# Letting an accumulating transfer make the low half of some weight pieces

## The chip, the cores and the metric

The kernel runs on one core of a Trainium2 chip. The metric is the device time of one execution in microseconds (us); three runs of the kernel as it stood took 2312.73, 2313.27 and 2313.78 us, so the time before is their median, 2313.27 us. The profile is a trace of one execution on that core.

## The reference

The program is a decoder trunk of two layers on 512 tokens of width 1024, all in float32. Each layer runs a half-step SwiGLU feed-forward, a token mixer (gated linear recurrence and differential attention in one layer, forgetting attention and a convolution in the other), cross-attention into 256 memory tokens, and a second feed-forward. Every sub-layer is normalised ahead and behind and added to the residual stream `h`. What matters here is the feed-forward:

```
def swiglu(x, w_gate, w_up, w_down):
    return (jax.nn.silu(x @ w_gate) * (x @ w_up)) @ w_down

def half_ffn(h, l, j):
    y = swiglu(rms_norm(h, ffn_norm_pre[l, j]), ffn_w_gate[l, j], ffn_w_up[l, j], ffn_w_down[l, j])
    return h + 0.5 * rms_norm(y, ffn_norm_post[l, j])
```

`w_down` is 2816 x 1024. There are four feed-forwards (two layers, two each).

## The kernel before

**Split products.** Every float32 matrix product is made of three products of rounded halves. A tensor X becomes a high part (X rounded to the `fp32r` format) and a low part (X minus the high part), and the result is high x low + low x high + high x high. So each weight piece goes through a small assembly line before TensorE (PE in the profile) can use it:

1. SyncE (the queue SPq) loads the raw piece, 128 partitions x 1024 floats (512 KB in two transfers of 256 KB), into one of 4 slots of `raw` (L541). It waits for the slot through the semaphore `lo_made`.
2. ScalarE (ACT) writes the rounded copy into one of 4 slots of `whi` (L791 for the pieces of this document), once the raw data is there and the piece that used the slot four pieces ago has been used by PE (`pieces_used`). It counts `hi_made`.
3. VectorE (DVE) writes raw minus high into `wlo` (L1319) and counts `lo_made`.
4. PE waits for `lo_made` (`weights`) and uses both; then it counts `pieces_used`.

ACT and DVE split three pieces ahead of the piece that PE is on (`LOOKAHEAD`). Each engine runs its own written-out order of work; the splits stand in it as calls of `split_next`.

**The plain down stage.** The feed-forward's down product is made in three stages; two use a fast block scheme, and the third, called `down` in the list of stages, is a plain product over the last 1280 rows of `w_down`. It has two groups (column halves of 512), each of 5 pieces. The document numbers its ten pieces 0 to 9: pieces 0 to 4 are the first group, 5 to 9 the second. A piece holds 2 x 128 rows; over the four token tiles it is 24 matmuls.

In the first group PE takes a piece for all four token tiles, then the next piece. In the second group (`last_group`) it takes piece 5 for all tiles, then pieces 6, 7, 8 and 9 for tile 0, then the same four for tile 1, then the rest. So pieces 6 to 9 are all wanted within one tile's time.

At the change of groups DVE runs `close_sublayer` in this order, one after the other: it waits until the first group is done, adds its four tiles to `y_rows` (L1460), splits piece 8, multiplies the four tiles by the gain (`gained`, L1471), splits piece 9, and then handles the second group's tiles as PE ends them. ACT splits piece 8, squares the four tiles (L841), and splits piece 9 once piece 5 is used. GpSimd (POOL) computes only reciprocal square roots in these stages (L692), each behind a wait.

Of the kernel before, what the change touches and what calls it, by code (L numbers as in the profile page):

```python
# [41 lines left out]
P = 128  # L42
# [7 lines left out]
RAW_SLOTS = 4  # L50
SPLIT_SLOTS = 4
# [39 lines left out]
def stages():  # L91

    out = []

    def ffn(l, j):
        for n, (_, ng) in enumerate(FF_GROUPS):
            out.append(("gate_up", l, (j, n), ng, KT // PK))
            if n < len(FF_GROUPS) - 1:
                out.append(("quads", l, (j, n), 1, len(quad_pieces())))
            else:  # L100
                out.append(("down", l, (j, n), 2, ng))
    for l in range(DEPTH):
        ffn(l, 0)
        out.append(("even_in", l, None, 7, 4) if l % 2 == 0 else ("odd_in", l, None, 6, 4))
        late = l % 2
        out.append(("kv", l, None, KV_GROUPS - late, 2))
        out.append(("mix_out", l, "late_kv" if late else None, 2, 4))
        out.append(("xq", l, None, 2, 4))
        out.append(("xo", l, None, 2, 4))
        ffn(l, 1)  # L110
    return out
# [16 lines left out]
def build(nc, A, out):  # L128
    f32, f32r, bf16, i8 = mybir.dt.float32, mybir.dt.float32r, mybir.dt.bfloat16, mybir.dt.int8
    ALU, ACT, AX = mybir.AluOpType, mybir.ActivationFunctionType, mybir.AxisListType  # L130
    MUL, ADD, SUB = ALU.mult, ALU.add, ALU.subtract
# [6 lines left out]
    def place(name, shape, dt=f32, at=None, size=FLOAT):  # L138

        n = (int(np.prod(shape[1:])) * size + 31) // 32 * 32  # L140
        if at is None:
            at = top[0]
            top[0] += n
        assert at + n <= nc.sbuf_usable_end, (name, at + n - nc.sbuf_usable_end)
        return nc.alloc_sbuf_tensor_at(name, shape, dt, offset=at)
# [9 lines left out]
    raw = place("raw", [P, RAW_SLOTS, PK, GC])  # L155
    whi = place("whi", [P, SPLIT_SLOTS, PK, GC], f32r)
    wlo = place("wlo", [P, SPLIT_SLOTS, PK, GC], f32r)
# [8 lines left out]
    ones = place("ones", [P, P])  # L166
# [11 lines left out]
    negmax = place("negmax", [P, 2, 2])  # L178
    rowsum = place("rowsum", [P, 2, 2])
    recip = place("recip", [P, 2, 2])  # L180
    lam = place("lam", [P, 8])
    tile_decay = place("tile_decay", [P, 4, TT])
    fbias = place("fbias", [FOX_HEADS, 8])
# [77 lines left out]
    flat = lambda t: t.rearrange("p a b -> p (a b)")  # L261
# [4 lines left out]
    def sem(name):  # L266
        return nc.alloc_semaphore(name)
# [5 lines left out]
    raw_full = [sem(f"raw_full{i}") for i in range(RAW_SLOTS)]  # L273

    hi_made, lo_made, pieces_used = map(sem, ("hi_made", "lo_made", "pieces_used"))

    bank_free = [sem("even_banks_free"), sem("odd_banks_free")]

# [44 lines left out]
    STAGES = stages()  # L323
# [22 lines left out]
    def group_pieces(kind, g, n, arg=None):  # L346

        return 1 if kind == "odd_in" and ODD_COLS[g][0] == "c_f" else \
            n + 2 if arg == "late_kv" and g == 0 else n

    total_pieces = sum(group_pieces(kind, g, n, arg) for kind, _, arg, ng, n in STAGES for g in range(ng))

    def column_name(kind, g):
        return {"even_in": EVEN_COLS, "odd_in": ODD_COLS}[kind][g][0] if kind in ("even_in", "odd_in") else ""

    def from_h(kind, arg):

        return kind in ("even_in", "odd_in", "xq") or (kind == "gate_up" and arg[1] == 0)
# [5 lines left out]
    def ends_sublayer(kind, arg):  # L364
        return kind in ("mix_out", "xo", "down")
# [11 lines left out]
    def scaled_rows(kind, l, arg):  # L377

        return kind == "gate_up" and (l, arg[0]) != (0, 0)

    def opens_scaled(n_stage):

        return n_stage + 1 < len(STAGES) and STAGES[n_stage + 1][0] == "gate_up"
# [11 lines left out]
    raw_of, raw_split, passes = [], [], []  # L395
# [52 lines left out]
    def unit_source(k, name, q):  # L448

        first_raw = passes[k][1]  # L450
        if name == "B22":
            return raw[:, (first_raw + q // 2) % RAW_SLOTS, q % 2, :]
        return {"B11": w11, "T3": w11, "B21": w21, "T4": w21, "T1": w12, "T2": w12}[name][:, q, :]

    piece_gain = []
    for kind, l, arg, ng, n in STAGES:
# [9 lines left out]
    def piece_rows(t, slot, n):  # L466

        return t[:, slot].rearrange("p a (b n) -> p (a b) n", n=PK * GC // n)
# [206 lines left out]
    def _(pool):  # L675
        E = Engine(pool, pool_step)
        g = nc.gpsimd
# [56 lines left out]
        for n_stage, (kind, l, arg, ng, np_) in enumerate(STAGES):  # L734
            base_piece = E.piece
            E.piece += sum(group_pieces(kind, g_, np_, arg) for g_ in range(ng))
            if from_h(kind, arg) and not scaled_rows(kind, l, arg):
                power(TT, 0, rstd_in, var_in)
            if base_piece == 0:
                power(MT, 8)  # L740
            if kind == "even_in":
                make_tables()


                power(16)
                for _ in range(4):
                    power(TT)
                E.made[ring_summed.name] += KT
                E.seen[ring_squared.name] += KT
            elif kind == "odd_in":  # L750
                E.await_(conv_ready)
                for c in range(1, CONV_T):
                    E.await_(conv_ready)
                    if c > 1:
                        E.own()
                    E.run(g.tensor_tensor(ring[:, 0, :], conv[:, 0, :] if c == 1 else ring[:, 0, :], conv[:, c, :],
                                          ADD), conv_added)
                power(TT)
                E.made[ring_summed.name] += CONV_T
                E.seen[ring_squared.name] += CONV_T  # L760
            elif ends_sublayer(kind, arg) and opens_scaled(n_stage):
                power(1, 0)
                input_power(0)
                power(1, 1)
                input_power(1)
                power(1, 2)
                power(1, 3)
                input_power(2)
                input_power(3)
            elif ends_sublayer(kind, arg):  # L770
                for t in range(TT):
                    power(1, t)
# [3 lines left out]
    def _(act):  # L776
        E = Engine(act, scalar_step)
        a = nc.scalar.activation

        def split(n):  # L780

            slot = n % SPLIT_SLOTS
            if raw_of[n] is None:
                split_units(n, slot)
                return
            from_slot = raw_of[n] % RAW_SLOTS
            act.wait_ge(raw_full[from_slot], 32 * (raw_of[n] // RAW_SLOTS + 1))
            act.wait_ge(pieces_used, n + 1)
            gains = piece_gain[n]
            if gains is None:  # L790
                a(flat(whi[:, slot]), flat(raw[:, from_slot]), ACT.Copy).then_inc(hi_made, 1)  # L791
                return
            hi, full = piece_rows(whi, slot, len(gains)), piece_rows(raw, from_slot, len(gains))
            for k, c in enumerate(gains):
                last = a(hi[:, k, :], full[:, k, :], ACT.Copy, scale=vec[:, c:c + 1])  # L795
            last.then_inc(hi_made, 1)
# [255 lines left out]
        for n_stage, (kind, l, arg, ng, np_) in enumerate(STAGES):  # L1052
            base_piece = E.piece
# [248 lines left out]
    def _(dve):  # L1302
        E = Engine(dve, vector_step)
        v = nc.vector

        def split(n):

            slot = n % SPLIT_SLOTS
            dve.wait_ge(hi_made, n + 1)
            if raw_of[n] is None:  # L1310
                k, units = units_at[n]
                for i, (name, q) in enumerate(units):
                    last = v.tensor_tensor(wlo[:, slot, i, :], unit_source(k, name, q), whi[:, slot, i, :].bitcast(f32), SUB)  # L1313
                last.then_inc(lo_made, 1)
                return
            from_slot = raw_of[n] % RAW_SLOTS
            gains = piece_gain[n]
            if gains is None:
                v.tensor_tensor(flat(wlo[:, slot]), flat(raw[:, from_slot]), flat(whi[:, slot]).bitcast(f32),  # L1319
                                SUB).then_inc(lo_made, 1)  # L1320
                return
            lo, hi, full = [piece_rows(t, at_slot, len(gains)) for t, at_slot in ((wlo, slot), (whi, slot), (raw, from_slot))]
            for k, c in enumerate(gains):
                last = v.scalar_tensor_tensor(out=lo[:, k, :], in0=full[:, k, :], scalar=vec[:, c:c + 1],  # L1324
                                              in1=hi[:, k, :].bitcast(f32), op0=MUL, op1=SUB)
            last.then_inc(lo_made, 1)
# [384 lines left out]
        for n_stage, (kind, l, arg, ng, np_) in enumerate(STAGES):  # L1711
            base_piece = E.piece
# [87 lines left out]
            for g in range(straight(kind, ng)):  # L1800
# [76 lines left out]
                else:  # L1877
# [4 lines left out]
                    scale = {"c_q": 0.125}.get(name, 0.0625 if kind == "xq" else None)  # L1882
# [3 lines left out]
                    elif kind == "xq" and g == 1:  # L1886
                        for half in range(2):
                            n = slice(2 * half, 2 * half + 2)
# [216 lines left out]
    def _(pe):  # L2105
# [300 lines left out]
        def weights(n):  # L2406

            pe.wait_ge(lo_made, n + 1 + RAW_SLOTS)

        def feature_major(slot, kp, n_kp, bank, src_hi, src_lo, k_of, n=SEQ):  # L2410

# [55 lines left out]
        for n_stage, (kind, l, arg, ng, np_) in enumerate(STAGES):  # L2467
# [41 lines left out]
            for g in range(straight(kind, ng)):  # L2509
# [24 lines left out]
                for n_piece in range(n_kp):  # L2534
                    kp = (0, 1, 0, 1, 2, 3)[n_piece] if late else n_piece
# [7 lines left out]
                    slot = E.piece % SPLIT_SLOTS  # L2543
# [267 lines left out]
```

## Time and profile before

| | |
|---|---|
| median of three runs | 2313.27 us (2312.73 to 2313.78) |
| span of the profiled execution, first to last instruction | 2311.2 us |
| what the median has beyond that span | 2.1 us |
| PE busy | 2289.0 us, 99% of the span |
| VectorE busy | 1336.2 us, 58% |
| ScalarE busy | 977.3 us, 42% |
| GpSimd busy | 73.6 us, 3% |
| the four plain down stages begin their second group at | 345.45, 1172, 1530 and 2276 us |

The busy time of PE is the union of pipelined matmuls; a 512-column matmul is drawn 389 ns long, but they begin every 227 ns. A wait of an engine is listed with the instruction that ended it. The profiled execution has no listed time of its own besides its span.

### The profile page before, as it was taken

The numbers are of one execution on the slowest core, as the hardware profiler recorded it, in microseconds if no ns is written. First come the engines' busy times: TensorE is split into PE (matmuls) and PEld (weight loads), VectorE is DVE, ScalarE is ACT, GpSimd is POOL, SyncE is SP. The second block draws the span as 40 slices with busy tenths as digits, with TensorE's granted clock in tenths as the row PEclk, the third lists the DMA queues.
The fourth block names the chain that finished last, engine by engine and source line by source line (L and its number), as shares of the span: only waits on it lengthen the run. The fifth ranks groups of instructions, "written<-read, shape, count | busy, mean of one in ns | idle before, by whom it ended". The sixth has DMA issues, their size and how long they took to land. (4 is left out here: it accounts for less than half of the span.)

```text
span 2311.2 us, 30089 instructions
## 1 busy us (share of the span) xinstructions
PE 2289.0 (99%) x11883; PEld 1940.0 (84%) x11883; DVE 1336.2 (58%) x1862; ACT 977.3 (42%) x1612; POOL 73.6 (3%) x115
## 2 busy tenths in 40 slices
PE   8999999999999999999999999999999999999998
PEld 7888888888888888888888888888878888888887
DVE  5857536596645646573355564346897574557334
ACT  5433324444444444443343433235266554444332
POOL 0000003000000000000010000000000000000000
PEclk9999999999999999999999999999999999999999
DMA  4332332311223223413323313333322222341321
GB/s 168 108 130 79 95 110 74 109 64 55 74 74 105 70 78 105 146 59 105 98 85 119 124 59 102 106 95 92 101 74 83 92 65 92 110 135 48 117 93 73
DMA packets 171650, 217.70 MB, mean 94 GB/s; under 512 B 13080, under 2 KB 123000, under 8 KB 171512
## 3 DMA queue, kind: packets, MB, share of 16 engines
q1 hardware_dynamic: 171400, 215.75, 29.0%
q8 instruction: 96, 1.57, 0.3%
q14 instruction: 42, 0.34, 0.0%
q10 hardware_dynamic: 112, 0.03, 0.0%
HBM read 213.63 MB, written 2.10 MB: 93 GB/s over the span
## 5 line engine op out<-in xcount | busy, mean ns | idle before, releaser
L2111 PE MATMUL ps<-xlo,whi 128*128 128x512 f32 (+1 forms) x2056 | 755.5, 367 | 2.1 <-DVE wlo L1324 2.1
L2112 PE MATMUL ps<-xhi,wlo 128*128 128x512 f32 (+1 forms) x2056 | 753.2, 366 | 0.0
L2113 PE MATMUL ps<-xhi,whi 128*128 128x512 f32 (+1 forms) x2056 | 753.0, 366 | 0.0
L1324 DVE SCALAR_TENSOR_TENSOR wlo<-raw,vec,whi 128x512 fp32r<-128x512 f32 (+1 forms) x488 | 340.8, 742 | 388.9 <-ACT whi L795 387.8
L795 ACT ACTIVATE whi<-raw,vec 128x512 fp32r<-128x512 f32 (+1 forms) x488 | 320.8, 709 | 445.4 <-PE ps L2113 390.5
L2111 PEld LDWEIGHTS ps<-xlo,whi 128*128 128x128 f32 x2056 | 388.6, 189 | 65.6 <-issue 2.7
L2113 PEld LDWEIGHTS ps<-xhi,whi 128*128 128x128 f32 x2056 | 388.4, 189 | 62.9
L2112 PEld LDWEIGHTS ps<-xhi,wlo 128*128 128x128 f32 x2056 | 388.6, 189 | 62.0
L1319 DVE TENSOR_TENSOR wlo<-raw,whi 128x1024 fp32r<-128x1024 f32 x104 | 126.7, 1223 | 183.1 <-ACT whi L791 182.3
L791 ACT ACTIVATE whi<-raw 128x1024 fp32r<-128x1024 f32 x104 | 109.5, 1057 | 199.7 <-PE ps L2113 199.3
L2111 PE MATMUL ps<-wlo,xhi 128*128 128x512 f32 x352 | 138.6, 394 | 1.0 <-issue 1.0
L2113 PE MATMUL ps<-whi,xhi 128*128 128x512 f32 x352 | 137.2, 390 | 0.0
L2112 PE MATMUL ps<-whi,xlo 128*128 128x512 f32 x352 | 137.1, 389 | 0.0
L2229 PE MATMUL ps<-wlo,mid_hi 128*128 128x512 f32 x336 | 131.6, 392 | 0.4 <-DVE wlo L1313 0.4
L2234 PE MATMUL ps<-whi,mid_hi 128*128 128x512 f32 x336 | 130.8, 389 | 0.0
L2233 PE MATMUL ps<-whi,mid_lo 128*128 128x512 f32 x336 | 130.8, 389 | 0.0
L2111 PE MATMUL ps<-wlo,plain_hi 128*128 128x512 f32 x320 | 125.0, 391 | 0.0
L2113 PE MATMUL ps<-whi,plain_hi 128*128 128x512 f32 x320 | 124.6, 389 | 0.0
L2112 PE MATMUL ps<-whi,plain_lo 128*128 128x512 f32 x320 | 124.5, 389 | 0.0
L814 ACT ACTIVATE whi<-w 128x512 fp32r<-128x512 f32 x144 | 83.3, 622 | 91.9 <-PE ps L2113 33.9
L1313 DVE TENSOR_TENSOR wlo<-w,whi 128x512 fp32r<-128x512 f32 x144 | 92.8, 685 | 35.3 <-ACT whi L814 34.4
L1752 DVE TENSOR_TENSOR mid<-mid,ps 128x1024 f32<-128x1024 f32 x33 | 40.3, 1221 | 111.9 <-ACT mid L1070 111.9
(291 smaller groups left out, 2909.5 us busy)
## 6 DMA issues: line engine op xcount, KB each, us to landing
raw<-ffn_w_gate_dram SPq DMA_DIRECT2D x176, 256.0 KB, 2.8
raw<-ffn_w_up_dram SPq DMA_DIRECT2D x176, 256.0 KB, 3.1
raw<-ffn_w_down_dram SPq DMA_DIRECT2D x96, 256.0 KB, 3.1
w<-ffn_w_down_dram SPq DMA_DIRECT2D x72, 256.0 KB, 5.3
raw<-xattn_w_kv_dram SPq DMA_DIRECT2D x64, 256.0 KB, 2.9
raw<-even_w_in_dram SPq DMA_DIRECT2D x56, 256.0 KB, 2.9
raw<-odd_w_in_dram SPq DMA_DIRECT2D x42, 256.0 KB, 2.9
raw<-xattn_w_q_dram SPq DMA_DIRECT2D x32, 256.0 KB, 3.0
```

The costliest lines, as they stand in the source:

```text
L791: a(flat(whi[:, slot]), flat(raw[:, from_slot]), ACT.Copy).then_inc(hi_made, 1)
L795: last = a(hi[:, k, :], full[:, k, :], ACT.Copy, scale=vec[:, c:c + 1])
L814: last = a(whi[:, slot, i, :], unit_source(k, name, q), ACT.Copy)
L1313: last = v.tensor_tensor(wlo[:, slot, i, :], unit_source(k, name, q), whi[:, slot, i, :].bitcast(f32), SUB)
L1319: v.tensor_tensor(flat(wlo[:, slot]), flat(raw[:, from_slot]), flat(whi[:, slot]).bitcast(f32), SUB).then_inc(lo_made, 1)
L1324: last = v.scalar_tensor_tensor(out=lo[:, k, :], in0=full[:, k, :], scalar=vec[:, c:c + 1], in1=hi[:, k, :].bitcast(f32), op0=MUL, op1=SUB)
L2111: mm(out_ap, lh, rl, start=start, stop=False, skip_group_check=skip_group_check)
L2112: mm(out_ap, ll, rh, start=False, stop=False, skip_group_check=skip_group_check)
L2113: return mm(out_ap, lh, rh, start=False, stop=stop, skip_group_check=skip_group_check)
L2229: opening = mm(out, hi, wlo[:, slot, i, :], start=fresh, stop=False, skip_group_check=True)
L2233: mm(out, lo, whi[:, slot, i, :], start=False, stop=False, skip_group_check=True)
L2234: last = mm(out, hi, whi[:, slot, i, :], start=False, stop=ends, skip_group_check=True)
```

## The change

Of the ten pieces of each plain down stage, every second of a group (pieces 1, 3, 6 and 8; 16 pieces in the kernel) gets its low part in another way. ACT first writes minus the raw piece, rounded, into `wlo`, and then the rounded copy into `whi`. When `hi_made` says so, GpSimd issues a transfer that adds the raw slot to `wlo` within SBUF (512 KB). When the transfer has landed (`raw_added`, one semaphore per slot), DVE copies one element per partition (`slot_marks`) and with it counts `lo_made`. PE waits for `raw_added` as well.

```
+    raw_added = [sem(f"raw_added{i}") for i in range(SPLIT_SLOTS)]
...
+                by_dma.append(kind == "down" and i % 2 == 1)
...
 # GpSimd, in the loop over stages
-            elif ends_sublayer(kind, arg) and opens_scaled(n_stage):
+            if kind == "down":
+                for g_ in range(ng):
+                    for kp in range(1, np_, 2):
+                        n = base_piece + np_ * g_ + kp
+                        slot, j = n % SPLIT_SLOTS, arg[0]
+                        pool.wait_ge(hi_made, n + 1)
+                        g.dma_start(wlo[:, slot], raw[:, raw_of[n] % RAW_SLOTS], accum_op=ADD).then_inc(raw_added[slot], 16)
+            if ends_sublayer(kind, arg) and opens_scaled(n_stage):
...
 # ScalarE, split
+            if by_dma[n]:
+                a(flat(wlo[:, slot]), flat(raw[:, from_slot]), ACT.Copy, scale=-1.0)
...
 # VectorE, split
+            if by_dma[n]:
+                dve.wait_ge(raw_added[slot], 16 * (added_before(n) + 1))
+                v.tensor_copy(slot_marks[:, slot:slot + 1], ones[:, 0:1]).then_inc(lo_made, 1)
+                return
...
 # TensorE, weights
+            if by_dma[n]:
+                pe.wait_ge(raw_added[n % SPLIT_SLOTS], 16 * (added_before(n) + 1))
```

## Rows read from the trace of the kernel before

**Rows 1.** The page, busy time of each engine: us, share of span, instructions.
```profile
PE 2289.0 (99%) x11883; PEld 1940.0 (84%) x11883; DVE 1336.2 (58%) x1862; ACT 977.3 (42%) x1612; POOL 73.6 (3%) x115
```

**Rows 2.** Waits of PE: engine, line, releaser, us in total, times, longest.
```profile
PE ps L2461 <- DMA rows<-xattn_norm_pre_dram: 7.1, 1, 7.1
PE ps L2111 <- DVE wlo L1324: 2.1, 2, 1.7
...
PE ps L2229 <- DVE wlo L1313: 0.4, 1, 0.4
```

**Rows 3.** Timeline of PE, first stage: start of pieces 0, 5 and 9.
```profile
318.25 0.39 PE L2111 MATMUL ps<-wlo,plain_hi 128*128 128x512 f32 x1
...
345.45 0.39 PE L2111 MATMUL ps<-wlo,plain_hi 128*128 128x512 f32 x1
...
354.98 0.39 PE L2111 MATMUL ps<-wlo,plain_hi 128*128 128x512 f32 x1
```

**Rows 4.** Timeline of ScalarE, first stage: start, us, instruction, idle before it.
```profile
307.63 1.06 ACT L791 ACTIVATE whi<-raw 128x1024 fp32r<-128x1024 f32 x1 [3.88 <-PE ps L2113]
...
323.24 2.00 ACT L791 ACTIVATE whi<-raw 128x1024 fp32r<-128x1024 f32 x2
...
334.83 1.06 ACT L791 ACTIVATE whi<-raw 128x1024 fp32r<-128x1024 f32 x1 [4.38 <-PE ps L2113]
...
345.71 1.06 ACT L791 ACTIVATE whi<-raw 128x1024 fp32r<-128x1024 f32 x1 [4.38 <-PE ps L2113]
...
351.15 1.06 ACT L791 ACTIVATE whi<-raw 128x1024 fp32r<-128x1024 f32 x1 [1.93 <-PE ps L2113]
```

**Rows 5.** Timeline of VectorE, first stage, at the change of groups.
```profile
345.65 2.48 DVE L1460 TENSOR_TENSOR y_rows<-ps,y_rows 128x512 f32<-128x512 f32 x4 [3.06 <-PE ps L2113]
348.28 1.23 DVE L1319 TENSOR_TENSOR wlo<-raw,whi 128x1024 fp32r<-128x1024 f32 x1
349.42 2.49 DVE L1471 TENSOR_TENSOR y_rows<-y_rows,post_gain 128x512 f32<-128x512 f32 x4
352.25 1.23 DVE L1319 TENSOR_TENSOR wlo<-raw,whi 128x1024 fp32r<-128x1024 f32 x1 [0.33 <-ACT whi L791]
356.53 0.69 DVE L1460 TENSOR_TENSOR y_rows<-ps,y_rows 128x512 f32<-128x512 f32 x1 [3.06 <-PE ps L2113]
358.02 0.16 DVE L1464 SCALAR_TENSOR_TENSOR var<-result_squares 128x1 f32<-128x1 f32 x1 [0.79 <-ACT y_scratch L841]
```

**Rows 6.** Timeline of VectorE, last stage, at the change of groups.
```profile
2276.74 2.48 DVE L1460 TENSOR_TENSOR y_rows<-ps,y_rows 128x512 f32<-128x512 f32 x4 [3.06 <-PE ps L2113]
...
2283.34 1.23 DVE L1319 TENSOR_TENSOR wlo<-raw,whi 128x1024 fp32r<-128x1024 f32 x1 [0.33 <-ACT whi L791]
```

**Rows 7.** Transfers by line: KB each, median us from issue to landing.
```profile
raw<-even_w_in_dram SPq DMA_DIRECT2D x56, 256.0 KB, 2.9
...
out_dram<-h SPq DMA_DIRECT2D x3, 512.0 KB, 2.6
mem_in<-mem_dram SPq DMA_DIRECT2D x1, 1024.0 KB, 6.8
```

**Rows 8.** Timeline of SyncE's queue, the reload behind piece 8.
```profile
349.54 0.80 SPq L541 DMA_DIRECT2D raw<-even_w_in_dram  x2
```

**Rows 9.** Windows of 1 us: busy time by engine, PE clock, DMA share, GB/s.
```profile
349.00:350.00 1.00, 1.00 (x7) 0.81 (x6) 1.00 (x2) 0.23 (x2) 0.00 (x0) 1.00 0.00 0
350.00:351.00 1.00, 1.00 (x6) 0.84 (x5) 1.00 (x3) 0.00 (x0) 0.00 (x0) 1.00 0.40 63
351.00:352.00 1.00, 1.00 (x6) 0.84 (x5) 0.92 (x2) 0.85 (x1) 0.00 (x0) 1.00 0.94 344
352.00:353.00 1.00, 1.00 (x6) 0.81 (x5) 0.75 (x1) 0.22 (x1) 0.00 (x0) 1.00 0.31 117
```

**Rows 10.** POOL by line: busy us, mean ns, idle before.
```profile
L756 POOL TENSOR_TENSOR ring<-ring,conv 128x512 f32<-128x512 f32 x2 | 3.5, 1752 | 59.3 <-DVE conv L1684 59.3
```

**Rows 11.** Timeline of POOL, first stage.
```profile
358.25 0.93 POOL L692 TENSOR_TENSOR rstd<-var,neg_half 128x1 f32<-128x1 f32 x1 [317.28 <-DVE var L1464]
```

More of the change, by code:

```diff
@@ L180, in build @@
     recip = place("recip", [P, 2, 2])
+    slot_marks = place("slot_marks", [P, SPLIT_SLOTS])
     lam = place("lam", [P, 8])
@@ L453, in unit_source, with added_before @@
         return {"B11": w11, "T3": w11, "B21": w21, "T4": w21, "T1": w12, "T2": w12}[name][:, q, :]
+    by_dma = []
+    for kind, _, arg, ng, n in STAGES:
+        for g in range(ng):
+            for i in range(group_pieces(kind, g, n, arg) if kind != "quads" else n):
+                by_dma.append(kind == "down" and i % 2 == 1)
+    assert len(by_dma) == total_pieces
+    def added_before(n):
+        return sum(by_dma[m] for m in range(n % SPLIT_SLOTS, n, SPLIT_SLOTS))
     piece_gain = []
```

## The prediction

> **What bounds the kernel now.** I read the busy times first, because a change that takes work from one engine and gives it to others is worth only what the bounding engine was waiting for. TensorE is busy 99% of the span, VectorE 58%, ScalarE 42%, GpSimd 3% [rows 1]. The second view is TensorE's own waits, since only they can be won back. The largest is 7.1 us for a first load at the start. On the low halves that VectorE makes it waits 2.1 and 0.4 us in the whole kernel [rows 2], and neither of these is L1319, the line that makes the low parts of the plain down stage. So nothing that VectorE gives up there can shorten the kernel by more than about nothing. The question is only whether the new route is late anywhere.
>
> The third view is therefore the timeline, to see when each piece is made and when TensorE wants it. From the start of piece 5 at 345.45 to that of piece 9 at 354.98 are 42 matmuls (24 of piece 5, then 6 each of pieces 6, 7, 8) [rows 3], so one takes 9.53 / 42 = 0.227 us, a piece 24 x 0.227 = 5.44 us, and a piece's share of one tile 6 x 0.227 = 1.36 us. The first group keeps this rhythm from 318.25 to 345.45, five pieces in 27.2 us [rows 3].
>
> **Where there is slack and where there is none.** In the first group ScalarE splits piece n when piece n-4 is used, three pieces ahead, 16.3 us before TensorE wants it. In the second group pieces 6 to 9 are wanted 1.36 us apart: piece 8 at 354.98 - 1.36 = 353.6 and piece 9 at 354.98, with the weight load some 0.2 us before (the pitch of one matmul, an estimate), so 354.8. VectorE ends the low part of piece 8 at 349.51 and that of piece 9 at 352.25 + 1.23 = 353.48 [rows 5]. Piece 9 has 1.3 us to spare, and its low part stands behind piece 8's in VectorE's order, with the four gain products between. The last stage has the same spacing: adds at 2276.74, piece 9's low part at 2283.34, 6.60 us later, as in the first stage (352.25 - 345.65) [rows 5, 6]. The middle two begin their second group in the same way, so I count four equal places.
>
> **The change part by part.**
>
> *Taken from VectorE:* 16 subtractions of 1.23 us [rows 5], 19.7 us. They stood off the path; gain 0. *Added to VectorE:* 16 copies of one element per partition, by the nearest small instruction 0.16 us each [rows 5], and 16 waits for a landed transfer, which are the matter (below).
>
> *Added to ScalarE:* 16 copies of 1.06 us [rows 4], 17 us, each ahead of the high part, so `hi_made` comes about 1.0 us later (two in a row take 2.00 us [rows 4]). The idle time ahead of these splits, 3.9 to 4.4 us [rows 4], covers it everywhere except at piece 8, where the four squares follow; there the 1 us adds to the chain.
>
> *Added to GpSimd:* 16 issues, each behind a wait. Queued behind them stand only its square roots, the first at 358.25 [rows 11], long after piece 8's issue. Cost 0 unless that issue were later than 358.
>
> *Added to the transfers:* 16 of 512 KB, with the target read as well. At piece 8 the transfer engines are idle until the reload of 349.54 [rows 8, 9], which itself now waits for piece 8's mark, so they don't collide. That reload (piece 12) would start near 354 instead of 349.5; its 256 KB parts land 2.9 us after issue [rows 7], and ScalarE can split piece 12 only when piece 8 is used, near 370. Cost 0.
>
> *Added to TensorE:* a second wait per use of these pieces, 9 a stage. TensorE passes the existing waits with no idle time between them [rows 2]; I take 0.
>
> *The duration that decides.* Call L the time from the end of ScalarE's two copies to the moment VectorE sees the transfer landed. No transfer within SBUF, none that adds, and none issued by GpSimd is in this trace, so I bound it. Low end: 512 KB from SBUF by SyncE's queue land 2.6 us after issue [rows 7], so L = 2.6. High end: 1024 KB, the bytes of source and target read together, land after 6.8 us [rows 7]; with GpSimd's dearest single instruction among these rows, 1.75 us [rows 10], for making the descriptors, L = 8.6. Between them: the reload of 512 KB is issued at 349.54, its second part about 0.4 us later, half of the 0.80 us [rows 8], and lands 2.9 us after that [rows 7], 3.3 us in all. Its bytes keep all 16 transfer engines for 0.40 + 0.94 + 0.31 = 1.65 us [rows 9]; reading the target too adds the same again; and the issue by GpSimd I price as one of its short instructions, 0.93 us [rows 11]. L = 3.3 + 1.65 + 0.93 = 5.9 us. I take this, as it is built from the same bytes in the same stretch.
>
> *Piece 1.* ScalarE starts at 307.63 [rows 4] and ends both copies at 309.6; the transfer lands at 315.5. Wanted at 318.25 + 5.44 = 323.7. Hidden, 8 us to spare.
> *Piece 3.* Its copies start at 323.24 and end at 325.24 [rows 4]; landed at 331.1; wanted at 318.25 + 16.3 = 334.6. Hidden with 3.3 us to spare: it would need L over 9.2.
> *Piece 6.* Copies 334.83 [rows 4] to 336.8, landed 342.7, wanted at 350.9. Hidden. VectorE is free again before its adds at 345.65 [rows 5].
> *Piece 8.* The copies start at 345.71 [rows 4] and end at 347.71. VectorE has ended its adds at 348.13 [rows 5] and now stands at the wait for the transfer until 347.71 + L = 353.6, which is just when TensorE wants piece 8. Behind the waiting instruction are the four gain products (2.49 us) and piece 9's low part (1.23 us) [rows 5]. With the mark's 0.16 and about 0.2 of overlap between neighbours, piece 9 is ready 0.16 + 2.49 + 1.23 - 0.2 = 3.7 us after the landing, at 351.4 + L. ScalarE's half of piece 9, at 351.15 [rows 4], waits for piece 5 and is not later than before. TensorE wants piece 9 at 354.8. So it stalls s = 351.4 + L - 354.8 = **L - 3.4 us** in each stage: 2.5 us with L = 5.9.
>
> *What is late next.* TensorE has no later idle time in which to make the stall good (99% busy, and every wait of [rows 2] is spread in bits under 2 us except the first), and the instructions that end a sub-layer follow its tiles. So the stall comes through whole: 4 x 2.5 = 10 us.
>
> *The sum.* The profiled span, 2311.2 us, becomes 2321.2. The median of the runs is 2.1 us above that span; adding it gives **2323 us**, 0.4% slower.
>
> **A rule that speaks for a shorter transfer.** The Trainium skill (DMA: Bandwidth & Descriptors, "Anatomy of one DMA") states for transfers issued by GpSimd about 2.0 us plus bytes over 436 GB/s. By it, as an estimate, 512 KB take 3.2 us, L would be under 3.4, and the time would stay at 2313 us. No row here shows a transfer of that kind. On the other hand Collectives: The Full Stack, "The bandwidth ceiling", says that an add in the transfer needs two reads for each byte delivered and halves the rate; by both together, as an estimate, 4.4 us, a stall of 1.0 us a stage and 2317 us.
>
> **The rivals.**
>
> *The transfer is hidden.* If L is at most 4.5 us, each stall is at most 1.1 us, four make under 4.6 us, and the time is 2313 to 2317.9. For it: the 512 KB that leave SBUF in 2.6 us [rows 7], and idle transfer engines at 346 to 350 us. Against it: nothing in that row reads its target or passes through GpSimd. It decides from L = 3.4 down to nothing at all. This is the "not slower" case. Chance 0.21. The first rule of the Trainium skill quoted above (DMA: Bandwidth & Descriptors) would give this case.
>
> *The adding transfer is far slower than a copy.* If the adding passes fewer bytes a second than a copy, so that L is about 14 us, piece 3 is late as well: from L = 9.2 on in the first stage, 14 - 9.2 = 4.8 us; I take some 3.5 us for the others, where ScalarE does piece 3 a little earlier against the rhythm (an estimate). Each stage then loses L - 3.4 = 10.6 us at piece 9 too. Sum 4 x 10.6 + 4.8 + 3 x 3.5 = 58 us, 2371. For it: no row prices the adding. Against it: the 1024 KB row covers the doubled bytes at 6.8 us. Chance of L over 8.6 (2334 and up): 0.19.
>
> *A gain.* The freed 17 us of VectorE (19.7 - 16 x 0.16) shorten something. TensorE waits 2.5 us on low parts in all [rows 2], so the best is 2310.8 us, still within 0.2%. For more, a wait that the rows don't show would be needed. Chance 0.02.
>
> **How the numbers follow.** About 0.2%, 4.6 us, is what a measurement of this kernel can tell from no change. The forecast (L from 4.5 to 8.6, 2318 to 2334) has 0.58, its middle 2323. Faster 0.02, from the last rival. Within 0.2% 0.21, the hidden case. Slower 0.58 + 0.19 = 0.77. The low bound 2315 leaves out those cases of the hidden transfer with L under 3.8 and the gain, about 0.10; the high bound 2342 goes past L = 8.6 to about 10.5 (7.1 us a stage, 28 us, and 1 us at piece 3) and leaves out half of the slow case, about 0.10.
>
> **What the profile of the changed kernel would show.** Right: a new wait of TensorE at the first matmul of piece 9 (or 8), released by VectorE's L1319 line for wlo, four times, about 2.5 us each; VectorE idle 4 to 6 us after its four adds, ended by the transfer; the four gain products directly behind; waits of TensorE elsewhere unchanged, and none at pieces 1, 3 and 6. Wrong if: TensorE has no wait there (L under 3.4); it waits at piece 3 (L over 9.2); the low parts of other stages become late; the span grows by time before the first or after the last matmul, as by setting up GpSimd's queue, which no row prices; or TensorE's granted clock, 1.00 in these windows [rows 9], falls after the stalls.

## The result and the profile after

The changed kernel takes 2318.64 us (median of 8 runs, 2315.75 to 2320.90) against 2312.65 us for the kernel before (8 runs beside them, 2310.36 to 2313.78). The ratio is 1.0027, with a 95% interval of 1.0018 to 1.0037: 6.0 us slower. The profiled execution took 2318.61 us, with a span of 2316.8 us, 5.6 us longer than that of before. The ratios in this document leave out the one slow execution among all the runs, 7608.58 us of the kernel with the gain products first (its median without it is 2311.89 us), and can differ from the quotient of the two printed medians in the fourth decimal.

The busy times show no new bound: TensorE stays at 99%, VectorE gave up 17.7 us, ScalarE took 16.8, GpSimd 14.1 [rows 1].

```profile
PE 2289.9 (99%) x11883; PEld 1939.5 (84%) x11883; DVE 1318.5 (57%) x1862; ACT 994.1 (43%) x1628; POOL 87.7 (4%) x131
```

The waits of TensorE (engine, line, releaser; us in all, times, longest) have one new line, the second:

```profile
PE ps L2489 <- DMA rows<-xattn_norm_pre_dram: 7.2, 1, 7.2
PE ps L2137 <- DVE wlo L1345: 4.3, 4, 1.1
PE ps L2137 <- DVE wlo L1350: 2.3, 2, 1.9
```

L1345 is the subtraction that was L1319. It holds TensorE up four times; the other two lines are those of [rows 2], within 0.2 us. The timelines of the first stage show the place. First ScalarE's two copies of piece 8 (start, us, instruction, in brackets the idle time before it):

```profile
345.56 1.06 ACT L811 ACTIVATE wlo<-raw 128x1024 fp32r<-128x1024 f32 x1 [4.38 <-PE ps L2139]
346.52 1.04 ACT L813 ACTIVATE whi<-raw 128x1024 fp32r<-128x1024 f32 x1
```

GpSimd's issue of the adding transfer behind them:

```profile
347.86 0.87 POOL L780 DMA_DIRECT2D wlo<-raw  x1 [10.01 <-ACT whi L813]
```

VectorE, to be laid beside [rows 5] and, for the last line, [rows 6]:

```profile
345.50 2.48 DVE L1486 TENSOR_TENSOR y_rows<-ps,y_rows 128x512 f32<-128x512 f32 x4 [1.55 <-PE ps L2139]
352.32 0.15 DVE L1333 COPY slot_marks<-ones 128x1 f32<-128x1 f32 x1 [4.34 <-DMA wlo<-raw]
352.40 2.50 DVE L1497 TENSOR_TENSOR y_rows<-y_rows,post_gain 128x512 f32<-128x512 f32 x4
354.81 1.22 DVE L1345 TENSOR_TENSOR wlo<-raw,whi 128x1024 fp32r<-128x1024 f32 x1
...
2280.99 2.48 DVE L1486 TENSOR_TENSOR y_rows<-ps,y_rows 128x512 f32<-128x512 f32 x4 [2.76 <-PE ps L2139]
```

And TensorE, the last matmul of piece 8 and the first ones of piece 9:

```profile
354.59 0.39 PE L2139 MATMUL ps<-whi,plain_hi 128*128 128x512 f32 x1
356.08 0.50 PE L2137 MATMUL ps<-wlo,plain_hi 128*128 128x512 f32 x1 [1.11 <-DVE wlo L1345]
356.42 0.40 PE L2138 MATMUL ps<-whi,plain_lo 128*128 128x512 f32 x1
356.66 0.39 PE L2139 MATMUL ps<-whi,plain_hi 128*128 128x512 f32 x1
356.88 0.40 PE L2137 MATMUL ps<-wlo,plain_hi 128*128 128x512 f32 x1
```

The reader is to see one chain. ScalarE ends at 347.56, the transfer is seen landed at 352.32, so L = 4.76 us. Before, VectorE was at the gain products at 349.42 and at piece 9's low part at 352.25 [rows 5]; now it stands idle for 4.34 us and comes to piece 9 at 354.81. Piece 9 was due one pitch (the 0.227 us from one matmul's start to the next) behind the last matmul of piece 8, at 354.59 + 0.227 = 354.82, and starts at 356.08, 1.26 us late. The next three matmuls begin 0.34, 0.24 and 0.22 us apart, so 1.38 us are lost when the pitch is back.

The four places lose nearly the same. VectorE's adds at the change of groups begin, before and after, at 345.65 and 345.50, 1172.38 and 1173.58, 1530.32 and 1532.99, 2276.74 and 2280.99. The differences are -0.15, 1.20, 2.67 and 4.25, and 5.6 at the end of the span: steps of 1.35, 1.47, 1.58 and 1.35 us. They add up to 5.75 us. The stalls at piece 9, each with the slow matmuls right behind it, are some 1.4 us, 5.5 us in all, so they make up nearly the whole of it.

The transfers by line give the landing, and five windows of the first stage, the last three of them those of the transfer, what it took (busy shares of the engines, TensorE's granted clock, share of the 16 transfer engines, GB/s; a listed share can exceed 1):

```profile
wlo<-raw POOLq DMA_DIRECT2D x16, 512.0 KB, 4.4
```

```profile
347.00:348.00 1.00, 1.00 (x6) 0.82 (x5) 0.98 (x2) 1.00 (x3) 0.14 (x1) 1.00 0.45 168
348.00:349.00 1.00, 1.00 (x6) 0.83 (x5) 0.00 (x0) 1.00 (x5) 0.73 (x1) 1.00 0.01 2
349.00:350.00 1.00, 1.00 (x6) 0.84 (x5) 0.00 (x0) 1.00 (x4) 0.00 (x0) 1.00 0.86 172
350.00:351.00 1.00, 1.00 (x6) 0.81 (x6) 0.00 (x0) 0.03 (x2) 0.00 (x0) 1.00 1.11 221
351.00:352.00 1.00, 1.00 (x6) 0.84 (x5) 0.00 (x0) 1.00 (x1) 0.00 (x0) 1.00 0.68 131
```

It keeps all sixteen busy for 0.86 + 1.11 + 0.68 = 2.65 us. The granted clock is 1.00 here and in the windows behind the stall, in all four stages.

### The profile page after: what moved, and what is told of

Read it like the earlier page. It is cut to its first block and busy times, and to the rows that moved or that the text cites. A ratio compares the mean times of both kernels' runs of the same rounds, so it can differ in the third digit from the quotient of the medians.

```text
span 2316.8 us, 30121 instructions
## 1 busy us (share of the span) xinstructions
PE 2289.9 (99%) x11883; PEld 1939.5 (84%) x11883; DVE 1318.5 (57%) x1862; ACT 994.1 (43%) x1628; POOL 87.7 (4%) x131
## 3 DMA queue, kind: packets, MB, share of 16 engines
q8 instruction: 96, 1.57, 0.3%
## 5 line engine op out<-in xcount | busy, mean ns | idle before, releaser
L1345 DVE TENSOR_TENSOR wlo<-raw,whi 128x1024 fp32r<-128x1024 f32 x88 | 106.9, 1222 | 97.6 <-ACT whi L813 97.4
```

## The experiments

The theory: only the transfer of piece 8 costs anything, because VectorE waits for it in order ahead of the gain products and piece 9's low part; s = L - 3.4 in each of four stages. The rivals: that every transfer costs something wherever it stands; and, on the size of L, that the adding itself costs nothing and the issue by GpSimd and the completion are all of it. VectorE's copy that counts `lo_made` is called the mark of its piece. Each kernel is compared with the kernel before on the same chip.

**Pieces 1, 3 and 6 alone.**

```
-                by_dma.append(kind == "down" and i % 2 == 1)
+                by_dma.append(kind == "down" and 5 * g + i in (1, 3, 6))
...
 # GpSimd issues for the pieces that by_dma names
```

> Only pieces 1, 3 and 6 of each plain down stage go by the adding transfer; piece 8 is split on VectorE as before. My theory (all of the loss is TensorE's wait at piece 9, behind VectorE's wait for piece 8's transfer): no wait at piece 9, the time of the kernel before, 2312.7 us, within about 2 us. Rival (each transfer, each extra ScalarE copy or GpSimd's queue costs something wherever it stands): 12 of 16 transfers are left, so three quarters of the 6.0 us stay, 2317.1 us.

2311.52 us against 2311.55, ratio 1.0002 (0.9993 to 1.0011), with no wait at piece 9. Twelve of the sixteen transfers, with their ScalarE copies, marks and second waits of TensorE, cost nothing that can be measured.

**Piece 8 alone.** The same line with `5 * g + i == 8`.

> Only piece 8 of each plain down stage goes by the adding transfer, 4 in the kernel. My theory: the whole loss stays, four lags of 1.3 us and the few tenths around them, 2318 us. Rival (cost per transfer): a quarter of 6.0 us, 2314.2 us.

2317.64 us against 2311.55, ratio 1.0027 (1.0016 to 1.0038): four transfers carry the whole loss. TensorE's waits:

```profile
PE ps L2136 <- DVE wlo L1344: 4.5, 4, 1.3
```

**The gain products first.** In `close_sublayer`, VectorE's call for piece 8 is moved behind the four `gained`; all sixteen transfers stay.

```
-            split_next()
+            if kind != "down":
+                split_next()
...
+            if kind == "down":
+                split_next()
```

> All 16 transfers stay; on VectorE the four gain products stand ahead of the wait for piece 8's transfer instead of behind it. My theory: VectorE does the gain products while the transfer runs, piece 8's mark still comes at about 352.4 us in the first stage, piece 9's low part ends at about 353.7 us, before TensorE wants it at 354.6, and the time is that of the kernel before, 2312.7 us within about 2 us. Rival 1 (the wait is for the transfer itself, at piece 8): the wait of TensorE stays about 1.1 us a stage, 2318 us. Rival 2 (cost per transfer or for the queue): 2318 us with no wait of TensorE in these stages.

2312.18 us against 2311.55, ratio 0.9999 (0.9990 to 1.0008). VectorE's timeline:

```profile
347.93 2.50 DVE L1497 TENSOR_TENSOR y_rows<-y_rows,post_gain 128x512 f32<-128x512 f32 x4 [0.30 <-ACT y_scratch L863]
351.97 0.15 DVE L1333 COPY slot_marks<-ones 128x1 f32<-128x1 f32 x1 [1.55 <-DMA wlo<-raw]
352.04 1.22 DVE L1345 TENSOR_TENSOR wlo<-raw,whi 128x1024 fp32r<-128x1024 f32 x1
```

The transfer takes as long as before (issue at 347.51, mark at 351.97), but the 2.5 us of gain products now fill VectorE's wait, and piece 9's low part follows the mark at once. So the transfer's length costs only through the place of the wait in VectorE's order.

**One microsecond more ahead of piece 8's issue.** GpSimd does one small power of 1.03 us first (`slot_marks` is made twice as wide for its result).

```
+                        if (g_, kp) == (1, 3):
+                            g.tensor_tensor(slot_marks[:, 4:8], ones[:, 0:4], neg_half[:, 0:4], ALU.pow)
```

> As the changed kernel, but GpSimd does one small power instruction on 4 columns (about 1.0 us) between the wait and the issue of piece 8's transfer. My theory (stall = L - 3.4 us, nothing absorbs it): 1.0 us more in each of four stages, the wait of TensorE about 2.1 us a stage, 2322.6 us. Rival (the end of a sub-layer has slack that takes up a small delay, or the loss is not this chain): unchanged, 2318.6 us.

2324.74 us against 2311.55, ratio 1.0055 (1.0043 to 1.0068): 13.2 us lost, where the theory expected 10. The wait grew by 0.8 us a stage, from 4.3 to 7.5 us in all, and that is only 3.2 of the 7.2 us by which it is worse than the changed kernel. The rest is in the windows behind the wait:

```profile
PE ps L2139 <- DVE wlo L1347: 7.5, 4, 1.9
```

```profile
357.00:358.00 1.00, 1.00 (x4) 0.76 (x3) 0.00 (x0) 0.00 (x0) 0.00 (x0) 0.50 0.58 123
358.00:360.00 2.00, 2.00 (x6) 1.54 (x5) 0.69 (x1) 0.29 (x1) 0.00 (x0) 0.50 0.56 201
360.00:362.00 2.00, 2.00 (x10) 1.62 (x9) 0.99 (x3) 0.43 (x2) 0.94 (x1) 0.97 0.00 0
```

The first number behind GpSimd's share is the granted clock: 0.50, 1.2 instead of 2.4 GHz, for some 3.4 us. Matmuls begin every 0.43 us there instead of 0.227, and about 1.6 us are lost by the starts of the matmuls. It fell so behind the three waits of 1.89 us, in the first three stages, and not behind the fourth, of 1.85 us. Three times 1.6 is 4.8 us; with the 7.5 us of the waits and some 0.3 us of slow first matmuls behind each of the four, that is about the whole loss.

**The same with the gain products first.** Both edits together.

> The order of VectorE with the gain products first, and the delay of 1.0 us on GpSimd ahead of piece 8's issue. My theory: with the gain products first there are about 1.0 us to spare behind the mark, so the same delay that cost 4 us and more in the other order costs under 0.2 us a stage: 2312.7 us within 2 us. Rival (the delay itself costs, whatever the order): 4 us or more, 2316.7 us.

2313.12 us against 2311.37, ratio 1.0004 (0.9995 to 1.0013), no wait at piece 9. The microsecond that costs 7 us in the one order costs nothing in the other that these runs can tell from no change.

**A copy in place of the adding.** The transfer is the same without `accum_op=ADD`, so this kernel leaves out the adding and its low parts are not made.

```
-g.dma_start(wlo[:, slot], raw[:, raw_of[n] % RAW_SLOTS], accum_op=ADD)
+g.dma_start(wlo[:, slot], raw[:, raw_of[n] % RAW_SLOTS])
```

> The 16 transfers copy the raw slot over the low part instead of adding to it, so the low parts of these pieces hold the raw piece: the same bytes are written, the target isn't read. My theory (the adding costs the second read, about 1.0 us of the 2.65 us for which it keeps the transfer engines): L falls from 4.8 to about 3.8 us, TensorE's wait from 1.1 to about 0.2 us a stage, 1.5 to 2 us in all above the kernel before, 2314.5 us. Rival (L is issue and completion, the adding is free): L and the time stay, 2318.6 us.

2311.64 us against 2311.37, ratio 1.0002 (0.9993 to 1.0011). Its transfers by line, GpSimd, VectorE and windows:

```profile
wlo<-raw POOLq DMA_DIRECT2D x16, 512.0 KB, 2.9
```

```profile
347.89 0.54 POOL L780 DMA_DIRECT2D wlo<-raw  x1 [10.34 <-ACT whi L813]
```

```profile
350.78 0.15 DVE L1333 COPY slot_marks<-ones 128x1 f32<-128x1 f32 x1 [2.77 <-DMA wlo<-raw]
```

```profile
349.00:350.00 1.00, 1.00 (x6) 0.84 (x5) 0.00 (x0) 1.00 (x4) 0.00 (x0) 1.00 1.14 430
350.00:351.00 1.00, 1.00 (x7) 0.81 (x6) 0.22 (x2) 0.05 (x1) 0.00 (x0) 1.00 0.26 90
```

ScalarE ends at 347.59, so L = 350.78 - 347.59 = 3.19 us, just under 3.4, and the stall is gone, as the formula asks. The adding costs 4.76 - 3.19 = 1.57 us of L: 1.25 us of the transfer engines (2.65 against 1.40) and 0.33 us of GpSimd's issue (0.87 against 0.54). My expectation that 0.2 us of wait would remain in each stage, 1.5 to 2 us in all, was wrong, and so is the rival that adding is free.

**Piece 9 alone.** `5 * g + i == 9`, so that the late transfer is that of the last piece itself.

> Only piece 9 of each plain down stage goes by the adding transfer, 4 in the kernel; piece 8 is split on VectorE. ScalarE can start piece 9 only when piece 5 is used, so its two copies end at about 353.0 us in the first stage, the transfer lands at 357.8 us, and TensorE wants it at 354.8: a lag of 3.2 us a stage. If a wait only costs its own length: 13 us, 2326 us. If TensorE's granted clock falls to 0.50 after such a wait, as it did in three of four stages with a wait of 1.9 us (about 1.7 us lost each time): 5 us a stage, 20 us, 2332 us. Rival (cost per transfer): 4 of 16, 2314.2 us.

2331.99 us against 2311.37, ratio 1.0088 (1.0074 to 1.0102). The loss is 20.6 us, and the four waits are 12.2 us of it:

```profile
PE ps L2136 <- DVE slot_marks L1332: 12.2, 4, 3.1
```

In the first stage TensorE waits 3.13 us, and from 359 to 362 its granted clock is 0.50, as it is behind the waits of the third and fourth stage; behind that of the second, 3.02 us, it stays at 1.00. So the expectation with the fallen clock is met, and that of the waits alone is not. It had counted on four falls of about the same cost; there were three, the one in the third stage longer (0.50 from 1550 to 1556), so that the number fits so well is in part luck.

**Three microseconds more ahead of pieces 1, 3 and 6.** Three powers one after the other, some 3.2 us, ahead of the issues that should have slack.

```
+                        if (g_, kp) != (1, 3):
+                            for _ in range(3):
+                                E.run(g.tensor_tensor(slot_marks[:, 4:8], ones[:, 0:4], neg_half[:, 0:4], ALU.pow))
+                                E.own()
```

> As the changed kernel, with three small power instructions (about 1.05 us each with their waits, 3.2 us together) on GpSimd ahead of the issue for pieces 1, 3 and 6, and nothing ahead of piece 8's. My theory: with L = 4.8 + 3.2 = 8.0 us these pieces stay ahead of TensorE (piece 3 is late only from L = 9.2 on), so no new wait, and the time of the changed kernel, 2318.6 us, 6.0 above the kernel before. Rival (the length of every transfer counts, since VectorE stands at the wait): 12 transfers later by 3.2 us, some of it shows, 2325 us or more.

2324.75 us against 2311.37, ratio 1.0059 (1.0046 to 1.0071). This was a miss: no further loss was expected, and it is 13.4 us. Piece 8's issue is on time (347.64), but its landing is seen at 354.57, 6.9 us after the issue instead of 4.5. Each mark also frees a slot of `raw`, and SyncE's reloads, released later (345.67 instead of 342.84), now run beside piece 8's transfer. The next three runs take this apart.

**Late at pieces 1 and 3 alone.** The same powers where `(g_, kp) in ((0, 1), (0, 3))`. The theory here was that only piece 6's mark matters.

> The delay of 3.2 us ahead of the issue for pieces 1 and 3 alone. The kernel with the delay at 1, 3 and 6 took 2324.8 us and not 2318, with piece 8's transfer landing 2.3 us later than in the changed kernel though its issue was not later. My theory now (piece 6's late mark holds back the reload of its raw slot, and that reload and the next one then run on the transfer engines together with piece 8's transfer): delaying pieces 1 and 3 is harmless, 2318 us, 6 us above the kernel before, the wait of TensorE about 1.1 us a stage. Rival (any later transfer costs): some 4 us of the 7 more, 2322 us.

2323.71 us against 2311.73, ratio 1.0053 (1.0041 to 1.0066). Another miss, and that theory fell. SyncE's timeline, first of the changed kernel, then of this one:

```profile
330.00 3.07 SPq L554 DMA_DIRECT2D raw<-ffn_w_down_dram  x6
333.12 0.43 SPq L675 DMA_DIRECT2D post_gain<-ffn_norm_post_dram  x1
342.84 10.46 SPq L554 DMA_DIRECT2D raw<-even_w_in_dram  x6
```

```profile
332.25 3.07 SPq L554 DMA_DIRECT2D raw<-ffn_w_down_dram  x6
335.36 0.43 SPq L675 DMA_DIRECT2D post_gain<-ffn_norm_post_dram  x1
344.61 9.80 SPq L554 DMA_DIRECT2D raw<-even_w_in_dram  x6
```

VectorE's marks of pieces 3, 6 and 8 in this kernel:

```profile
332.06 0.15 DVE L1337 COPY slot_marks<-ones 128x1 f32<-128x1 f32 x1 [8.64 <-DMA wlo<-raw]
...
344.43 0.15 DVE L1337 COPY slot_marks<-ones 128x1 f32<-128x1 f32 x1 [9.94 <-DMA wlo<-raw]
...
353.43 0.15 DVE L1337 COPY slot_marks<-ones 128x1 f32<-128x1 f32 x1 [5.32 <-DMA wlo<-raw]
```

Piece 3's mark, with the two low parts that VectorE makes right behind it, releases six reloads in a row, and the load of the gains (`post_gain`, 512 KB) follows them in SyncE's queue. In the changed kernel they begin at 330.00, 7.0 us ahead of piece 6's issue at 336.98, which is marked 5.7 us after it. Here they begin at 332.25, 3.1 us ahead of piece 6's issue at 335.33, and that is marked at 344.43, 9.1 us after it. Its mark in turn releases the reloads of 344.61, only 1.6 us ahead of piece 8's issue at 346.21 (5.0 us in the changed kernel), and piece 8 is marked 7.2 us after its issue. So, by these times, the lateness is handed from piece to piece by SyncE's loads: from 3 to 6 by the reloads and the load of the gains, which no run separates, from 6 to 8 by reloads alone, which the next two runs test.

**Late at piece 6 alone.** The same where `(g_, kp) == (1, 1)`.

> The delay of 3.2 us ahead of the issue for piece 6 alone. My theory now (the held-back reloads meet piece 8's transfer): the whole of the loss returns, 2324.8 us, with piece 8 marked about 2 us later in the first stage and the transfer engines busy without a gap from piece 6's reload to that mark. Rival (any later transfer costs, piece 6 no more than 1 or 3): a third of the 7 more, 2320 us.

2323.24 us against 2311.73, ratio 1.0052 (1.0038 to 1.0065). Piece 6's mark comes at 344.88, piece 8's issue at 347.98, its mark at 353.28, 5.3 us later, and piece 9 waits 1.90 us. From issue to mark that is 0.8 us more than in the changed kernel, where a mark about 2 us later was expected; the time lies somewhat below the expected 2324.8 us and above the rival's 2320. The transfer engines, idle at 0.01 from 348 to 349 in the changed kernel, are not idle here:

```profile
348.00:349.00 1.00, 1.00 (x6) 0.84 (x5) 0.56 (x1) 1.00 (x5) 0.84 (x1) 1.00 0.83 195
349.00:350.00 1.00, 1.00 (x6) 0.81 (x5) 0.00 (x0) 1.00 (x4) 0.00 (x0) 1.00 0.94 293
```

**Late at piece 6, and the reloads behind it held back.** SyncE's next reloads wait for piece 8's mark.

```
+            for back in (2, 3):
+                m = raw_split[n] - back
+                if m >= 0 and by_dma[m] and not by_dma[m - 1] and not any(by_dma[m + 1:m + 4]):
+                    sp.wait_ge(lo_made, m + 1 + RAW_SLOTS)
```

> The kernel with the delay of 3.2 us at piece 6 alone, and SyncE holds back the reloads for the next two pieces (10 and 11) until piece 8 is marked, so that no load runs beside piece 8's transfer; ScalarE needs those pieces only some 10 us later. My theory (a late mark does harm only through the reloads that it releases, which meet the next adding transfer on the transfer engines): piece 8's transfer lands about 4.8 us after its copies again, TensorE's wait is about 1.1 us a stage, and the time that of the changed kernel, 6 us above the kernel before, 2318 us. Rival (a late piece 6 delays VectorE's and ScalarE's work at the change of groups by itself): 2323 us as without the hold.

2318.56 us against 2312.58, ratio 1.0022 (1.0013 to 1.0032): back at the loss of the changed kernel, though the mark of piece 6 (343.36) is as late as in the run before, 3.1 us ahead of piece 8's issue in both. VectorE's mark of piece 8, SyncE and TensorE's wait:

```profile
350.89 0.15 DVE L1341 COPY slot_marks<-ones 128x1 f32<-128x1 f32 x1 [3.85 <-DMA wlo<-raw]
```

```profile
351.14 3.82 SPq L558 DMA_DIRECT2D raw<-even_w_in_dram  x7
```

```profile
PE ps L2145 <- DVE wlo L1353: 4.3, 4, 1.1
```

The reload starts behind the mark, the issue of 346.45 is marked 4.4 us later, and the four waits are again 4.3 us. So piece 6's late mark harms piece 8 only through the reloads that it releases.

No version beats the kernel before. Pieces 1, 3 and 6 alone, or all four with the gain products first, equal it.

## Why the prediction came out as it did

**Mechanism and place: right.** Piece 9 waits behind the gain products, four times alike, and no other piece waits anew. Leaving out piece 8 removed the loss, and piece 8 alone kept it.

**The formula: right.** L = 4.76 gives s = 1.36 us; 1.26 was measured at the first matmul and 1.38 once the pitch was back. The threshold is bracketed from below too: with L = 3.19 there was no wait. The formula gives the stall; that the time grows by no more than the stall holds only where the clock does not fall (below).

**What was costed at nothing: right for this kernel.** The 17.7 us of VectorE bought nothing, the copies of ScalarE and the second waits of TensorE cost nothing, the stall came through whole. ScalarE has no idle time ahead of its split of piece 3 [rows 4], so that copy was not covered by idle time, as was said, but by the time to spare. At piece 8 the transfer engines are indeed idle when it starts (0.01 from 348 to 349), but barely. The prediction had them idle from 346 on, as they are in the kernel before (0.00 in each window from 346 to 350); in the changed kernel piece 6's mark at 342.66 holds the reloads back to 342.84, and they are still at 0.45 from 347 to 348. That these did not meet piece 8's transfer was not worked out, and is in part luck.

**The term that was mis-sized: L, 5.9 us taken, 4.76 measured.** I summed a reload's time to landing, 3.3 us, a second read, 1.65, and an issue by GpSimd, 0.93. The second read was close (adding cost 1.57 us). The copy was not: with its issue by GpSimd it took 3.19 us in all, where I had 3.3 + 0.93 = 4.2. A reload's 2.9 us are counted from its issue and so hold one already, and I added another. So each stall was taken as 2.5 us and is 1.4; four times 1.1 is the 4.4 us between 2323 and 2318.6. With L at 4.76 the result lies at the forecast's low edge: the hidden case was bounded by L = 4.5, and the ratio's interval reaches down to 1.0018. The high bound of L, 8.6, was far off.

The Trainium skill (DMA: Bandwidth & Descriptors, "Anatomy of one DMA") gave, as an estimate, 3.2 us for 512 KB issued by GpSimd; the copy, which landed 2.9 us after its issue, is near it, the adding transfer at 4.4 us is not. With the Trainium skill's rule of two reads (Collectives: The Full Stack, "The bandwidth ceiling"), which the page states for collectives, the estimate was 4.4 us and 2317 us; the trace agrees with its 4.4 us, and shows the halved rate: 221 GB/s in a window that the adding transfer fills, 430 for the copy. L is longer than these 4.4 us, because it begins where ScalarE ends, 0.30 us before the issue (347.56 to 347.86).

**A step whose ground was too narrow.** For pieces 1, 3 and 6 I asked only when TensorE wants the piece, and found 3.3 us to spare at piece 3. But the mark also frees the raw slot. Delays of 3.2 us at pieces for which TensorE did not come to wait cost 5.5 to 7.4 us more than the changed kernel loses, through loads that met the next adding transfer (tested at piece 6 by holding them back, read from the times at pieces 1 and 3). The spare time of such a transfer ends where the loads that it releases would run into piece 8's, and that is earlier. In the changed kernel itself this cost nothing that was shown: the loss with piece 8 alone is as large.

**The clock.** It was named as something that would make the prediction wrong, without a price. Behind waits of 1.1 us it did not fall; behind seven of twelve waits of 1.9 us it did. The sum with L = 5.9 and stalls of 2.5 us would have needed that price: in the run with one microsecond more ahead of piece 8's issue, L is 352.57 - 346.99 = 5.58 us in the first stage, the formula gives 4 x 2.2 = 8.7 us, and the loss was 13.2. That the sum came out without the price is owed to the shorter L.

**What stays open.** The runs with late marks lost 11.5 to 13.4 us. Their traces, from the first matmul of the first plain stage to the end, are 12.0 us (late at 1, 3 and 6), 15.2 (at 1 and 3) and 9.1 (at 6) longer than that of the kernel before. The waits at pieces 8 and 9 (8.1, 8.9 and 6.8 us), some 0.28 us of slow first matmuls behind each (1.4, 1.7 and 1.1) and falls of the clock of about 1.6 us each (one, two and one) come to 11.1, 13.8 and 9.5 us. What is left is within what executions differ by: every one of these traces, that of the kernel before too, has a stretch of granted clock 0.50 near 590 us, outside these stages, and it lasts from about 7 to 14 us. Why the clock fell behind some waits of 1.9 and 3.0 us and not behind others of the same length was not tried.

## What to carry to other kernels

A wait in an engine's fixed order costs what is queued behind it, so put the independent work ahead of it: here moving four products made a 6 us loss vanish. When work moves to a transfer, ask not only who uses its result but what its completion releases, and whether that runs into the next transfer. TensorE, 99% busy, hardly waited for the engine that was relieved here, so the change could at best come out even.

## What the runs showed of the hardware

An adding transfer of 512 KB within SBUF lands 4.4 us after GpSimd's issue and keeps the transfer engines for 2.65 us, a copy 2.9 us and 1.40 us. With loads running beside it, it took 5.3 to 9.1 us from issue until it was marked, instead of 4.4 to 4.5.

A short idle time of TensorE can cost more than its length. Behind waits of 1.06 to 1.3 us (eight of them) the granted clock stayed at 1.00. Behind twelve waits of 1.89 to 1.91 us in four kernels (one microsecond ahead of piece 8's issue, and late at pieces 1, 3 and 6, at 1 and 3, and at 6) it fell to 0.50 seven times, and behind four of 2.98 to 3.13 us three times. One such fall behind a wait of 1.89 us cost about 1.6 us of TensorE's time.
